# Sum of squares of a gated SSD group: the three squared tiles are added on GpSimd ahead of one product of ones, and carried rows are scaled ahead of the next decay products

## The reference, cut to what matters

```python
y_diag = jnp.einsum("bclsgr,bcsgrp->bclgrp", cb[..., None] * decay, xdt)
y_off = jnp.einsum("bclgn,bcgrpn->bclgrp", cc, h_enter) * jnp.exp(a_cum)[..., None]
return y_diag + y_off
...
y = (y + d_skip[..., None] * xs).reshape(b, l, SSD_INNER) * jax.nn.silu(z.astype(jnp.float32))
yg = y.reshape(b, l, SSD_GROUPS, SSD_INNER // SSD_GROUPS)
yg = yg * lax.rsqrt(jnp.mean(yg * yg, axis=-1, keepdims=True) + NORM_EPS)
```

## Time and profile before

| | before |
|---|---|
| runs (3) | median 1197.61 us, 1197.46 to 1197.94 |
| profiled execution | 1197.97 us, span 1196.2 us |
| TensorE busy | 97% of the span |
| VectorE, ScalarE busy | 70%, 52% |
| GpSimd busy | 7% |
| mean granted TensorE clock | 0.997 of full speed |

### The profile page before, as it was taken

The page is one execution under the profiler, slowest core; times in us unless marked ns, Lnnn a source line. Parts: engine busy times, 40 slices in busy tenths (PEclk is TensorE's granted clock), DMA queues, the critical chain, the costliest instruction groups (busy, mean ns, idle before and its releaser), DMA issues.

```text
span 1196.2 us, 17207 instructions
## 1 busy us (share of the span) xinstructions
PE 1160.4 (97%) x6430; PEld 931.2 (78%) x6430; DVE 840.1 (70%) x1208; ACT 616.8 (52%) x1074; POOL 84.4 (7%) x73
## 2 busy tenths in 40 slices
PE   5999999999999999999999999999999899999998
PEld 3667677787777787887887887887887579998997
DVE  4563677887978656893882882897777977754655
ACT  5541484848574546621421421446854777654553
POOL 0000101010010043000000000044000004000000
PEclk9999999999999999999999999999999999999999
DMA  9856543332322233643633633632333005455554
GB/s 362 343 182 218 194 126 108 106 124 80 123 80 80 88 114 103 244 142 126 230 138 128 232 131 132 231 129 71 124 133 132 2 2 176 159 186 184 191 180 156
DMA packets 49893, 179.13 MB, mean 150 GB/s; under 512 B 5216, under 2 KB 7584, under 8 KB 47776
## 3 DMA queue, kind: packets, MB, share of 16 engines
q1 hardware_dynamic: 49536, 177.66, 43.5%
q10 hardware_dynamic: 288, 0.56, 0.1%
HBM read 177.05 MB, written 1.15 MB: 149 GB/s over the span
## 4 chain that ended last, share of the span: by engine, by line
PE 80%; DVE 8%; ACT 7%; DMA 2%; issue 2%; SPq 0%; DVEq 0%; ACTq 0%
PE ps L1929 51%; PE ps L1936 9%; PE ps L2223 6%; ACT ey L1268 3%; PE ps L2021 2%; PE ps L1952 2%; DVE sm L1877 1%; ACT ey L1271 1%; DMA mhalf<-in_w_mod 1%; DVE prob L1902 1%; PE ps L2134 1%; DVE ycomb L1709 1%; PE ps L2341 1%; DMA xload<-in_ctx 1%; ACT mixF L1255 1%
## 5 line engine op out<-in xcount | busy, mean ns | idle before, releaser
L1412 DVE TENSOR_TENSOR w_lo<-raw,w_hi 128x1024 fp32r<-128x1024 f32 x206 | 261.9, 1272 | 89.1 <-ACT w_hi L1042 89.0
L1042 ACT ACTIVATE w_hi<-raw 128x1024 fp32r<-128x1024 f32 x206 | 216.7, 1053 | 191.3 <-DMA raw<-in_w_ff 154.6
L1929 PE MATMUL ps<-a_hi,w_hi 128*128 128x512 f32 (+1 forms) x820 | 299.2, 365 | 0.0
L1929 PE MATMUL ps<-a_hi,w_lo 128*128 128x512 f32 (+1 forms) x820 | 288.9, 352 | 0.0
L1929 PE MATMUL ps<-a_lo,w_hi 128*128 128x512 f32 (+1 forms) x820 | 288.7, 352 | 0.0
L1929 PEld LDWEIGHTS ps<-a_hi,w_hi 128*128 128x128 f32 x820 | 155.1, 189 | 25.1 <-issue 2.7
L1929 PEld LDWEIGHTS ps<-a_lo,w_hi 128*128 128x128 f32 x820 | 155.1, 189 | 23.2 <-issue 1.0
L1929 PEld LDWEIGHTS ps<-a_hi,w_lo 128*128 128x128 f32 x820 | 155.0, 189 | 21.3
L1929 PE MATMUL ps<-b_hi,w_hi 128*128 128x512 f32 x304 | 119.2, 392 | 0.0
L1929 PE MATMUL ps<-b_lo,w_hi 128*128 128x512 f32 x304 | 118.5, 390 | 0.0
L1929 PE MATMUL ps<-b_hi,w_lo 128*128 128x512 f32 x304 | 118.3, 389 | 0.0
(11 more groups left out here) (289 smaller groups left out, 1762.0 us busy)
## 6 DMA issues: line engine op xcount, KB each, us to landing
raw<-in_w_ff SPq DMA_DIRECT2D x128, 512.0 KB, 3.5
mring<-in_w_mod SPq DMA_DIRECT2D x32, 768.0 KB, 5.2
raw<-in_w_in_even SPq DMA_DIRECT2D x36, 512.0 KB, 5.5
mring<-in_w_mod SPq DMA_DIRECT2D x16, 1024.0 KB, 5.1
ey<-acum_rows SPq DMA_DIRECT2D x32, 384.0 KB, 5.1
raw<-in_w_in_odd SPq DMA_DIRECT2D x18, 512.0 KB, 3.5
mhalf<-in_w_mod SPq DMA_DIRECT2D x16, 512.0 KB, 9.7
raw<-in_w_out_even SPq DMA_DIRECT2D x16, 512.0 KB, 3.5
```

The source lines that it names most:

```text
L1042: nc.scalar.activation(w_hi[:, u % RING, :, :], raw[:, u % RING, :, :], ACT.Copy).then_inc(hi_done, 1)
L1412: v.tensor_tensor(w_lo[:, u % RING, :, :], raw[:, u % RING, :, :], w_hi[:, u % RING, :, :].bitcast(F32), ALU.subtract).then_inc(lo_done, 1)
L1929: ins = mm(out_ap, w_[:, n % RING, k, :], (x_[k][:, 0:ntok] if type(x_) is list else x_[:, k, 0:ntok]), start=(k == 0 and j == 0), stop=(k ...
```

## The change

Three edits of the step list and of the `ysum` step:

- For groups 0, 1 and 3, GpSimd adds the three squared tiles (two additions of 128x512, each waiting for the one before), and TensorE makes one product of ones where it made three. Group 2 keeps three products.
- The `ysum` of groups 0 and 1 moves: it stood between the third and the fourth `state` of the next group, now it stands after slot 1 and `xskip`. Their `ynorm` moves from after slot 1 to after slot 2.
- In groups 0, 1 and 2 the `seg f` of the next chunk comes behind `yt` and `yoff` of this one, not ahead of them.

```diff
-        if g:
+        if g == G - 1:
             s.append(("ysum", g - 1))
         states(3, 3)
...
-        if g:
+        if g == G - 1:
             s.append(("ynorm", g - 1))
+        elif g:
+            s.append(("ysum", g - 1))
         mixsplits(0, 1)
         for n in range(NCH):
-            if n < NCH - 1 and not last:
-                s.append(("seg", g, "f", ch[n + 1]))
             if n:
                 s.append(("yt", g, ch[n - 1]))
             s.append(("yoff", g, ch[n]))
+            if n < NCH - 1 and not last:
+                s.append(("seg", g, "f", ch[n + 1]))
...
             slot(2 + n)
+            if n == 0 and 0 < g < G - 1:
+                s.append(("ynorm", g - 1))
...
+        summed = {g: i + 1 for i, g in enumerate(g for g in range(G) if g != G - 2)}
...
+                elif st[0] == "ysum" and st[1] in summed:
+                    pool.wait_ge(ysq_done, st[1] + 1)
+                    pool.tensor_tensor(gate[:, 0, :], gate[:, 0, :], gate[:, 1, :], ALU.add).then_inc(pair_sq, 1)
+                    pool.wait_ge(pair_sq, summed[st[1]])
+                    pool.tensor_tensor(gate[:, 0, :], gate[:, 0, :], gate[:, 2, :], ALU.add).then_inc(group_sq, 1)
...
-                    for i in range(XT):
-                        ins = mm(ps[:, b, :], ones, gate[:, i, :], start=(i == 0), stop=(i == XT - 1))
+                    parts = 1 if st[1] in summed else XT
+                    if st[1] in summed:
+                        pe.wait_ge(group_sq, summed[st[1]])
+                    for i in range(parts):
+                        ins = mm(ps[:, b, :], ones, gate[:, i, :], start=(i == 0), stop=(i == parts - 1))
```

More of the change, by code:

```diff
@@ L686, in trunk @@
         rows_in = [[sem(f"rows_in{i}{d}") for d in "fb"] for i in range(3)]
-        names = ("arow_done rows_out coef_half grow_done htok_done unit_done sines_done hv_done mfull_done dtrow_done acc_sq tmp_sq mu_used row_done mcol_done modc_done sil_done hi_done lo_done c0_in dft_in xsq_done xrms_done xr_done xn_done xnt_done xu_done c1_in vec_in wdt_in bias_in dve_seq act_seq consts_set vt_done "
+        names = ("pair_sq group_sq arow_done rows_out coef_half grow_done htok_done unit_done sines_done hv_done mfull_done dtrow_done acc_sq tmp_sq mu_used row_done mcol_done modc_done sil_done hi_done lo_done c0_in dft_in xsq_done xrms_done xr_done xn_done xnt_done xu_done c1_in vec_in wdt_in bias_in dve_seq act_seq consts_set vt_done "
                  "silc_done th0_done h_done sq_done var_done rstd_done nt_done u_done split_done coef_done "
@@ L696, in trunk @@
         S = {n: sem(n) for n in names}
-        (arow_done, rows_out, coef_half, grow_done, htok_done, unit_done, sines_done, hv_done, mfull_done, dtrow_done, acc_sq, tmp_sq, mu_used, row_done, mcol_done, modc_done, sil_done, hi_done, lo_done, c0_in, dft_in, xsq_done, xrms_done, xr_done, xn_done, xnt_done, xu_done, c1_in, vec_in, wdt_in, bias_in, dve_seq, act_seq,
+        (pair_sq, group_sq, arow_done, rows_out, coef_half, grow_done, htok_done, unit_done, sines_done, hv_done, mfull_done, dtrow_done, acc_sq, tmp_sq, mu_used, row_done, mcol_done, modc_done, sil_done, hi_done, lo_done, c0_in, dft_in, xsq_done, xrms_done, xr_done, xn_done, xnt_done, xu_done, c1_in, vec_in, wdt_in, bias_in, dve_seq, act_seq,
          consts_set, vt_done, silc_done, th0_done, h_done, sq_done, var_done, rstd_done, nt_done,
```

## The result

The changed kernel takes **1213.84 us** (median of 4 runs, 1211.55 to 1214.40), the kernel before 1197.78 beside it (4 runs, 1197.46 to 1198.01): ratio 1.0126, 95% interval 1.0113 to 1.014. It is slower, as forecast, but by 16.1 us and not by 7.4, and the time lies above the range of 1198.0 to 1209.5. The profiled execution took 1214.24 us, span 1212.5 us, mean granted clock 0.992; the one before 1197.97, 1196.2 and 0.997.

The account below looks back on a forecast made before the run. TensorE was taken as the bound, with 80% of the chain. The terms, -3.8 + 2 x (0.9 + 1.0 + 3.2) + 0.8 = +7.2, gave 1205.2 from the profiled 1197.97, rounded to 1205.0 us; range 1198.0 to 1209.5.

Parts of the forecast that it names:

- Part 1: Groups 0 to 2: yt and yoff ahead of seg f remove TensorE's six waits for carried rows, -3.8 us.
- Part 2: Groups 0 and 1: removing products ahead of the fourth state gains 0; the product behind slot 1 costs +0.9 us each.
- Part 3: GpSimd's additions delay VectorE's w_lo, and with it the hent copies and fourth to sixth state, +1.0 us per group.
- Part 4: Groups 1 and 2: moved Ln, Exp and ynorm delay seg b, so TensorE waits at y1, +3.2 us each.
- Part 5: Group 3: the sum directly follows a gemm and waits for GpSimd's additions, +0.8 us, between -0.1 and +1.7.
- rival 3: The granted clock falls behind each new 3.2 us wait at y1, giving 1211.8 us; chance 0.04.

Follow-up runs that it names:

- the experiment: The kernel before with only seg f of the next chunk moved behind yt and yoff in groups 0 to 2: 1194.34 us.
- all waits filled: The changed kernel with throwaway TensorE products in its waits at the fourth state and y1 (groups 1, 2) and at group 3's sum: 1207.36 us.
- the product in the old place: Kernel before with seg f moved, plus GpSimd additions and single product for sums of groups 0 and 1, still ahead of the fourth state: 1199.98 us.
- TensorE kept busy: The changed kernel with four throwaway products ahead of the fourth state and four ahead of y1's decay products, in groups 1 and 2: 1208.07 us.

## Why the prediction was half right

**The direction and, within some tenths each, the queues were right.** Measured at full clock or with the additions left out, the terms stand:

- Part 1, carried rows, forecast -3.8 us: the experiment gives 1198.12 - 1194.34 = 3.8, and group 0 of the changed kernel ends 1.13 us earlier (forecast 1.2 to 1.3).
- Part 2, products taken from ahead of the fourth state gain nothing: right. The fourth state waits for the `hent` copy in any case, 2.7 us with no additions.
- Part 3, `w_lo` 1.0 us later beside GpSimd: 0.8 us in the changed kernel.
- Part 4, a wait of 3.2 us at y1: 3.6 us, with the releaser that was named, and a wait of VectorE for seg f over 4 us (7.57). With all waits filled the last chunks of groups 0, 1 and 2 come at 181.68, 254.10 and 326.94 us; so groups 1 and 2 are 4.1 and 4.5 us longer than before, where 3.9 each was forecast.
- Part 5, +0.8 us: a wait of 2.58 and 1.1 us in all, inside its bounds.

Together they give about 1207.5 and not 1205.2. Against the terms, the profiled execution with all waits filled, 1207.62, is 0.2 and 0.6 longer in groups 1 and 2, 0.7 in group 3 with its sum and 0.2 behind; and its last chunk of group 0 comes 0.6 later than forecast, nearly all of it because its scan began 0.5 later (137.32 and not 136.81). Each is small, and together they are a quarter of the miss.

**What failed is Part 2's sentence that TensorE "waits there until 206.9", at no cost, and rival 3's 0.04.** The sum was by queues alone, at full clock. I had two kinds of long wait in my own forecast, 2.7 to 3.7 us in the states of groups 1 and 2 and 3.2 us at y1, in a stretch where the kernel before had none over 1 us. For such a wait the only row was the earlier trace rows, where the clock was 0.75 behind waits. I gave that 4 in 100, because the scan showed no case; but the scan could not show one, since the waits were new. The clock is worth about 6.5 us of the 16.1 (1213.84 - 1207.36 with all waits filled). Two things show that it is the clock and not the queues: products behind the waits take 1.62 and 2.83 us where they took 0.88 and 1.53, and with fillers, at the same delays, they take 0.91 and 1.53.

Rival 3's time, 1211.8, is the nearest of all to the measured one, and its term of 6.8 us the nearest to 6.5, but by luck. It was priced for the two waits at y1 alone, at 3.4 us each; there were falls at four waits, of 0.9, 2.1, 2.6 and 1.6 us. And the 3.4 us of the earlier trace rows were no loss: the changed kernel's profiled execution has a clock of 1.00 from 0 to 100 us (before 0.97), and its scan begins at 136.88, before at 136.81.

**What stays open:** why one wait of 3.48 us has full speed behind it and the same wait in another execution half, and why the same wait's fall costs 0.9 us in one group and 2.1 in the next. In the profiled execution without GpSimd's additions two waits of 2.7 us and two of 2.0 had full speed behind them. Nothing was run that moves a wait in time without changing its length. Of each kernel but one execution has a profile, so how often a fall comes is known only from the times.

## What to carry to other kernels

A wait on TensorE had two prices here: its length, and the lower clock on what stands behind it. If a change opens waits like those here, 2.6 to 3.6 us on a TensorE that was 97% busy before, the second price was between nothing and 2.7 us for each; count it even if the trace of before shows no such fall, for it has no such wait. Work that "was hidden anyway" under another engine's chain may be what keeps the clock up: taking it out gains nothing, and can lose, 0.9 and 2.1 us at the two fourth states here. And when a change has two halves, price each by itself: here one half alone was worth 3.8 us.

## What the runs showed that was not expected

Whether the clock falls behind a wait of 2.6 to 3.6 us differs from one place and execution to the next. With the product in the old place it makes two heaps in the times, 1198.55 to 1199.29 us at a mean clock of 0.997 or 0.998 and 1200.67 to 1202.19 at 0.994. The wait of 2.58 us ahead of the sum of group 3 had full speed behind it in the changed kernel's profiled execution, and 0.86 from 400 to 412 us in that of "TensorE kept busy". And throwaway products in a wait are worth having: 19 of them took 6.5 us off a kernel of 1213.84, which is still 9.4 slower than the kernel before, because the waits themselves stay.
